# GpSimd's low parts in one instruction of 512 columns, weights released in halves, moments from a sum, and new orders at both ends of a two-block kernel

## The reference, cut to what matters

```
h  = rms_norm(x) * (1 + scale) + shift        # shift, scale, gate: cond @ w_mod
z  = h @ w_in                                  # a_glu, a_val, a_gate, b_q, b_k, b_v, ..., c_gate
u  = conv31(a_val * sigmoid(a_glu)) + b        # 256 channels, one filter of 31 taps each
u  = (u - mean(u)) * rsqrt(mean((u - mean(u))^2) + eps) * ln_w + ln_b   # moments over 256 channels
out = concat(u * gate, window_attention, gated_linear_attention) @ w_out
x  = x + gate * out
```

## Time and profile before

| | before |
|---|---|
| median of 3 runs | 3510.61 us (3509.44 to 3516.84) |
| profiled execution, its own time | 3512.96 us |
| its span, first to last instruction | 3510.8 us |
| mean granted TensorE clock | 0.983 of full speed |
| PE busy | 3364.6 us, 96% of the span |
| DVE / ACT / POOL busy | 60% / 32% / 62% |

### The profile page before, as it was taken

How to read it: one execution, slowest core, us unless ns; L and a number is a source line. 1 busy time by engine, 2 the same in 40 slices (tenths; PEclk the granted TensorE clock), 3 DMA queues, 4 the chain that set the end, 5 groups by cost and what they waited for, 6 DMA issues and landing times.

```text
span 3510.8 us, 51803 instructions
## 1 busy us (share of the span) xinstructions
PE 3364.6 (96%) x19544; PEld 2701.0 (77%) x19544; DVE 2107.1 (60%) x2913; ACT 1131.7 (32%) x1875; POOL 2188.3 (62%) x2500
## 2 busy tenths in 40 slices
PE   5999999999999999999899999998999989999997
PEld 3787688878778777878678888877887768888875
DVE  5684734469652465335766666664534576666666
ACT  4114744221663332232422222233223232222222
POOL 3354433667543578458866667777646886666774
PEclk9999999999999999999999999999999999999998
DMA  5511011332100343224211111123313411111112
GB/s 219 222 60 37 2 37 45 115 125 61 31 21 25 112 147 97 55 67 133 78 43 55 54 55 55 55 79 102 91 55 91 131 58 40 55 55 55 55 37 78
DMA packets 98696, 261.84 MB, mean 75 GB/s; under 512 B 9232, under 2 KB 34832, under 8 KB 97680
## 3 DMA queue, kind: packets, MB, share of 16 engines
q1 hardware_dynamic: 80048, 215.53, 18.5%
q10 hardware_dynamic: 18400, 43.00, 4.2%
HBM read 228.09 MB, written 16.78 MB: 70 GB/s over the span
## 4 chain that ended last, share of the span: by engine, by line
PE 84%; DVE 8%; POOL 3%; ACT 2%; issue 2%; DMA 1%; SPq 0%; ACTq 0%; DVEq 0%; POOLq 0%
PE banks L835 12%; PE banks L837 12%; PE banks L836 12%; PE banks L1376 7%; PE banks L1375 7%; PE banks L1374 7%; PE banks L1414 4%; PE banks L1416 4%; PE banks L1415 4%; PE banks L960 2%; PE banks L977 2%; PE banks L991 2%; POOL w_lo L2977 2%; DVE nt L2266 1%; POOL w_hi L2975 1%
## 5 line engine op out<-in xcount | busy, mean ns | idle before, releaser
L835 PE MATMUL banks<-h_hi,w_hi 128*128 128x512 f32 (+1 forms) x2160 | 838.6, 388 | 20.0 <-POOLq L2982 16.5
L837 PE MATMUL banks<-h_hi,w_lo 128*128 128x512 f32 (+1 forms) x2160 | 818.8, 379 | 0.0
L836 PE MATMUL banks<-h_lo,w_hi 128*128 128x512 f32 (+1 forms) x2160 | 817.7, 379 | 0.0
L2977 POOL TENSOR_TENSOR w_lo<-raw,w_hi 128x256 fp32r<-128x256 f32 x792 | 728.4, 940 | 31.7
L2975 POOL CAST w_hi<-raw 128x512 fp32r<-128x512 f32 x396 | 311.1, 786 | 570.6 <-PE banks L837 407.1
L835 PEld LDWEIGHTS banks<-h_hi,w_hi 128*128 128x128 f32 x2160 | 408.2, 189 | 109.5 <-POOLq L2982 21.3
L836 PEld LDWEIGHTS banks<-h_lo,w_hi 128*128 128x128 f32 x2160 | 408.3, 189 | 82.7 <-issue 6.7
L837 PEld LDWEIGHTS banks<-h_hi,w_lo 128*128 128x128 f32 x2160 | 407.9, 189 | 79.5
L1414 PE MATMUL banks<-g_slot,w_hi 128*128 128x512 f32 x704 | 281.2, 399 | 10.4 <-DVE g_slot L2860 7.3
L1416 PE MATMUL banks<-g_slot,w_lo 128*128 128x512 f32 x704 | 278.8, 396 | 0.0
L1415 PE MATMUL banks<-g_slot,w_hi 128*128 128x512 f32 x704 | 277.9, 395 | 0.0
(11 more groups left out here) (300 smaller groups left out, 6054.2 us busy)
## 6 DMA issues: line engine op xcount, KB each, us to landing
raw<-w_in SPq DMA_DIRECT2D x118, 512.0 KB, 3.5
raw<-w_out SPq DMA_DIRECT2D x64, 512.0 KB, 3.5
pair_y<-w_ffn SPq DMA_DIRECT2D x20, 1024.0 KB, 5.1
raw<-w_ffn SPq DMA_DIRECT2D x20, 1024.0 KB, 5.0
x<-w_mod SPq DMA_DIRECT2D x16, 1024.0 KB, 6.6
wk<-residual ACTq DMA_DIRECT2D x42, 256.0 KB, 2.8
piece<-w_down SPq DMA_DIRECT2D x40, 256.0 KB, 3.0
nt<-w_down SPq DMA_DIRECT2D x40, 256.0 KB, 2.8
```

Source lines behind the costliest of these rows:

```text
L835: mm(o, wh[:, ws], hi[:, kt, t0:t0 + n], start=kt == 0, stop=False)
L836: mm(o, wh[:, ws], lo[:, kt, t0:t0 + n], start=False, stop=False)
L837: last = mm(o, wl[:, ws], hi[:, kt, t0:t0 + n], start=False, stop=kt == nk - 1)
L2977: last = G.tensor_tensor(w_lo[:, piece], raw[:, piece], w_hi[:, piece].bitcast(F32), ALU.subtract)
```

## The change

1. **GpSimd.** The subtract that makes `w_lo` is one instruction of 512 columns where two of 256 stood (L2977 and L3131).
2. **Halves.** `w_split` counts halves: GpSimd raises it after either half, and PE waits for the half that it is to read. In `project` the order is half by half over the token chunks, except for the first block's in-projections (chunk by chunk).
3. **Start.** The parts of `w_mod` are loaded in another order, so that shift and scale of tiles 0 to 3 are complete after two parts. Turns go in pairs into two PSUM banks, DVE's modulation is done in two halves, each followed by its four tiles, and ACT's squares for p1 stand behind all its roundings.
4. **Moments.** In layer 0 of the first block DVE adds the two convolved tiles, and the two squared tiles, before PE's moment matmuls, which are six instead of twelve each time.
5. **End of the feed-forward part.** For the last f, ACT's `take_first` stands ahead of a first tap and a `round_g`, `take_u` behind a first tap; DVE's `low` of the first half stands ahead of the second half's taps, and four additions of the unit down10 p0 are pulled up between the taps.

The diff, cut to its core:

```
-                    for piece in (slice(c, c + 256), slice(c + 256, c + 512)):
-                        last = G.tensor_tensor(w_lo[:, piece], raw[:, piece], w_hi[:, piece].bitcast(F32), ALU.subtract)
+                    last = G.tensor_tensor(w_lo[:, c:c + 512], raw[:, c:c + 512], w_hi[:, c:c + 512].bitcast(F32), ALU.subtract)
+                    if half == 0:
+                        last.then_inc(sem["w_split"], 1)
                 link(last)
...
-                        for c in (0, 256):
-                            part = G.tensor_tensor(w_lo[:, o + c:o + c + 256], src[:, c:c + 256], w_hi[:, o + c:o + c + 256].bitcast(F32), ALU.subtract)
+                        part = G.tensor_tensor(w_lo[:, o:o + 512], src, w_hi[:, o:o + 512].bitcast(F32), ALU.subtract)
...
-                pe.wait_ge(sem["w_split"], g + 1)
+                steps = [(half, ci) for half in range(2) for ci in some]
+                if SEQ[g][0] == "in1":
+                    steps = [(half, ci) for ci in some for half in range(2)]
+                for half, ci in steps:
+                    pe.wait_ge(sem["w_split"], 2 * g + 1 + half)
...
+    START_MOD = [0, 8, 4, 12]
+    TURN_BANKS = [7, 5]
...
-                if u:
-                    turn_modulation(u - 1, 4, mod_row[:, (u - 1) * 512:u * 512], 4 * (u - 1))
+                if u in (1, 3):
+                    turn_modulation(u - 1, 4, mod_row[:, (u - 1) * 512:u * 512], START_MOD[u - 1], u // 2)
                 if u == 1:
                     mean_square(0, 0)
-            turn_modulation(3, 4, mod_row[:, 1536:2048], 12)
+                if u in (1, 3):
+                    turn_modulation(u, 4, mod_row[:, u * 512:(u + 1) * 512], START_MOD[u], u // 2)
...
-            dve.wait_ge(sem["wm_turned"], 4)
-            modulation(0, 0, 16, psum[7][:, 0:32])
-            dve.wait_ge(sem["mod_ready"], 1)
-            tiles(0, 0, range(DT))
+            for half in range(2):
+                dve.wait_ge(sem["wm_turned"], 2 * half + 2)
+                modulation(0, 4 * half, 4 * half + 4, psum[TURN_BANKS[half]][:, 8 * half:8 * half + 8])
+                modulation(0, 8 + 4 * half, 12 + 4 * half, psum[TURN_BANKS[half]][:, 16 + 8 * half:24 + 8 * half])
+                tiles(0, 0, range(4 * half, 4 * half + 4))
...
+                if l == 0:
+                    link(V.tensor_tensor(cv_sq[0][:, 0:end], cv_a[0][:, 0:end], cv_a[1][:, 0:end], ALU.add))
+                    dve.sem_inc(sem["conv_ready"], 1)
...
                 rope(0, at_k)
+                if l == 0:
+                    dve.wait_ge(sem["cstat_ready"], 2)
+                    link(V.tensor_tensor(cv_sq[0][:, 0:end], cv_sq[0][:, 0:end], cv_sq[1][:, 0:end], ALU.add))
+                    dve.sem_inc(sem["cent_ready"], 1)
                 rope(1, at_q[0])
...
-                        last = mm(psum[CONV_BANKS[ci]][:, 0:w], k("ones256"), cv_a[j][:, t0:t0 + w], start=j == 0, stop=j == 1)
+                        last = mm(psum[CONV_BANKS[ci]][:, 0:w], k("ones256"), (cv_a[j] if l else cv_sq[0])[:, t0:t0 + w], start=j == 0, stop=j == l)
...
+                first_tap(NF - 2, 0, 0)
+                first_tap(NF - 2, 1, 0)
+                gate_silu(NF - 2, 0)
+                take_first(NF - 1)
+                first_tap(NF - 2, 0, 1)
+                round_g(NF - 2, 0)
+                gate_silu(NF - 2, 1)
+                first_tap(NF - 2, 1, 1)
+                take_u(NF - 1)
...
+                    if f == NF - 1:
+                        adds += [(len(UNITS) - 3, d, True) for d in range(EARLY_ADDS)]
...
-                    taps_(0)
+                    if f < NF - 1:
+                        taps_(0)
                     low()
+                    if f == NF - 1:
+                        taps_(0)
                     taps_(1)
```

More of the change, by code:

```diff
@@ L823, in project @@
                 _, _, _, nk, chunks, _ = SEQ[g]
-                pe.wait_ge(sem["w_split"], g + 1)
                 wh, wl = w_hi[:, (g % 2) * 1024:], w_lo[:, (g % 2) * 1024:]
-                for ci, (t0, n) in enumerate(chunks):
-                    if only is not None and ci != only:
-                        continue
+                some = range(len(chunks)) if only is None else [only]
+                steps = [(half, ci) for half in range(2) for ci in some]
[3 more added lines that the diff above has]
+                    pe.wait_ge(sem["w_split"], 2 * g + 1 + half)
+                    t0, n = chunks[ci]
                     q = FIRST_CHUNK[g] + ci
-                    if q >= 3:
+                    if q >= 3 and half == 0:
                         pe.wait_ge(sem[f"acc_free{q % 3}"], q // 3)
                     o = (psum_of(q) if bank is None else psum[bank])[:, 0:n]
-                    for kt in range(nk):
+                    for kt in range(4 * half, 4 * half + 4):
                         ws = slice(kt * P, (kt + 1) * P)
@@ L837, in project @@
                         last = mm(o, wl[:, ws], hi[:, kt, t0:t0 + n], start=False, stop=kt == nk - 1)
-                        if kt == 3 and ci == len(chunks) - 1:
-                            last.then_inc(sem["half_used"], 1)
-                    last.then_inc(sem["acc_ready"], 1)
+                    if half:
+                        last.then_inc(sem["acc_ready"], 1)
+                    elif ci == len(chunks) - 1:
+                        last.then_inc(sem["half_used"], 1)
             def project_some(g, ci, k0, k1):
@@ L866, in modulate, with turn_modulation @@
                 last.then_inc(sem["wm_used"], 1)
-            def turn_modulation(n, count, row, m0):
+            def turn_modulation(n, count, row, m0, half=0):
                 pe.wait_ge(sem["wm_copied"], n + 1)
                 for m in range(count):
-                    last = mm(psum[7][:, 2 * (m0 + m):2 * (m0 + m) + 2], row[:, m * P:(m + 1) * P], k("pick"), start=True, stop=True)
+                    last = mm(psum[TURN_BANKS[half]][:, 2 * (m0 + m):2 * (m0 + m) + 2], row[:, m * P:(m + 1) * P], k("pick"), start=True, stop=True)
                 last.then_inc(sem["wm_turned"], 1)
@@ L1523, in _ @@
             copy_row(2)
+            act.wait_ge(sem["mod_ready"], 1)
+            round_h(0, 0, 0)
+            round_h(0, 0, 1)
             copy_row(3)
-            act.wait_ge(sem["mod_ready"], 1)
-            for j in range(4):
+            round_h(0, 0, 2)
+            round_h(0, 0, 3)
+            act.wait_ge(sem["mod_ready"], 2)
+            for j in range(4, DT):
                 round_h(0, 0, j)
             act.wait_ge(sem["x_in1"], 16)
[L1529 to L1532, removed]
+            for d in range(DT):
                 square(0, 1, d, x)
@@ L2181, in _ @@
                 take_c12(F0 + 1)
-                for f in range(F0 + 2, NF):
+                for f in range(F0 + 2, NF - 1):
                     first_tap(f - 1, 0, 0)
@@ L2195, in _ @@
                     take_c12(f)
+                first_tap(NF - 2, 0, 0)
[7 more added lines that the diff above has]
+                take_u(NF - 1)
+                round_g(NF - 2, 1)
+                take_p7(NF - 1)
+                take_c11(NF - 1)
+                take_c12(NF - 1)
                 for h in range(2):
@@ L2834, in add_some @@
                     def add_some():
-                        for n, c in itertools.islice(adds, each):
-                            take_down(n, c)
+                        for n, c, final in itertools.islice(adds, each):
+                            take_down(n, c, final)
                     def taps(m):
@@ L2867, in whole @@
                 def whole(f, n=None):
-                    adds = iter([(n, c) for c in range(U_RESULT[n + 1] - U_RESULT[n])] if n is not None else [])
+                    adds = [(n, c, None) for c in range(U_RESULT[n + 1] - U_RESULT[n])] if n is not None else []
+                    if f == NF - 1:
+                        adds += [(len(UNITS) - 3, d, True) for d in range(EARLY_ADDS)]
+                    adds = iter(adds)
                     each = 2 if f == F0 + 1 else 1
@@ L2881, in whole @@
                     low_()
-                    for n, c in adds:
-                        take_down(n, c)
+                    for n, c, final in adds:
+                        take_down(n, c, final)
                 def take_c22(f):
```

50 lines of the change are left out of this document (29 added, 21 removed).

## The result

The changed kernel takes 3528.77 us (median of 6 runs, 3517.70 to 3529.70), the kernel before 3510.03 (6 runs, 3502.69 to 3516.84). The ratio of the means is 1.0044 with a 95% interval of 1.0025 to 1.0062: it is slower by about 0.44% (0.53% by the medians), where 0.54% faster was forecast. The time lies in the rival that had 0.06 (3523 us): the long subtract costs DVE its critical chains.

The account below looks back on a forecast made before the run. PE, busy 96% of the span, was taken as the bound. Terms −1.6 − 5.0 − 4.25 − 3.7 − 4.4 = −18.95, say −19, from the median 3510.61 gave 3491.6 us; 8 in 10 for 3482 to 3503.

Parts of the forecast that it names:

- the rival that had 0.06: Feed-forward starts and norms: the long subtract costs critical DVE instructions 0.3 us each, net +13, 3523 us; chance 0.06.
- part 1: The 512-wide subtract on POOL: 0.13 us less per half; cost to DVE zero where saturated, 0.145 us each elsewhere.
- Part 6: Other norms and waits: DVE chains beside POOL's splits change by −0 us, within ±2 over all.
- Part 2: Two feed-forward starts: halves let PE start earlier, DVE pays 2 us in the chain; −0.8 each, −1.6 us both.
- Part 3: The start: first half's modulation and tiles come earlier, so norm and later wait shift; −5.0 us.
- Part 4: Moments of layer 0: six matmuls instead of twelve, twice, with DVE's additions covered; −4.25 us.
- Part 5: Two feed-forward ends: PE's waits of 2.31 and 3.64 us go, the second paying partly; −3.7 and −4.4 us.
- the lock: DVE instructions with two SBUF inputs and POOL instructions reading SBUF exclude each other; charged 2 us per feed-forward start.

Follow-up runs that it names:

- e3: The changed kernel with four subtracts of 128 columns instead of one of 512; 3525.33 us, ratio 1.0036 to the kernel before.
- e1: The changed kernel with the subtract back in two instructions of 256 columns everywhere; 3490.31 us, ratio 0.9936 to the kernel before.
- e11: e1 with the copy for the high part of the projections' blocks cut into two of 256; 3491.16 us, ratio 0.9937.
- e8: e1 without halves: PE waits for both halves of a block before its first matmul; 3498.56 us, ratio 0.9963.
- e9: e1 with the feed-forward ends in the order of the kernel before; 3493.83 us, ratio 0.9947.
- e10: e1 with the new orders but no additions of the unit down10 p0 pulled up; 3490.97 us, ratio 0.9935.
- e2: The kernel before with only the 512-wide subtract; 3543.14 us, ratio 1.0084.
- e6: e1 with 512-wide subtracts only in 92 projection blocks (start, norms, feed-forward starts); 3513.09 us, ratio 1.0003.
- e7: e1 with four subtracts of 128 in 15 blocks (start, layer 1's norms, second layers' start); 3495.54 us, ratio 0.9950.

## Why the prediction was wrong

**The step that failed is in part 1**: "On average that is zero where DVE is saturated (what it loses is POOL's time in total, 1.28 for 1.41)". It took POOL's work in a stretch as fixed. But DVE's work in a critical stretch is what is fixed, a number of tiles, and POOL, which had a backlog, does as many turns beside it as DVE has instructions. The price of a DVE instruction is then set by POOL's mean turn. POOL's instructions, min, median and max ns, in the changed kernel, e3, e1 and e11:

```profile
L3019 POOL TENSOR_TENSOR w_lo<-raw,w_hi x396: 1262/1300/3227, 35.6 to 2843.4; 128x512 fp32r<-128x512 f32 x198
L3018 POOL CAST w_hi<-raw x396: 606/613/3195, 34.9 to 2842.2; 128x512 fp32r<-128x512 f32 x198
```

```profile
L3020 POOL TENSOR_TENSOR w_lo<-raw,w_hi x1584: 445/462/2511, 35.1 to 2848.0; 128x128 fp32r<-128x128 f32 x198
```

```profile
L3020 POOL TENSOR_TENSOR w_lo<-raw,w_hi x792: 717/742/2782, 35.1 to 2816.4; 128x256 fp32r<-128x256 f32 x198
```

```profile
L3018 POOL CAST w_hi<-raw x396: 386/398/2172, 34.3 to 2812.6; 128x256 fp32r<-128x256 f32 x198
```

Mean turn from the minima, and half of a tile (one DVE instruction):

```
                          POOL's turns of a half     mean turn   DVE instruction
four subtracts of 128     0.61 + 4 x 0.445            0.48        0.90
two of 256, copy cut      2 x 0.386 + 2 x 0.717       0.55        0.98
two of 256                0.61 + 2 x 0.717            0.68        1.12
one of 512                0.61 + 1.262                0.93        1.42
```

From the first row to the last the turn grows by 0.45 us and the DVE instruction by 0.52; the two rows between lie on that line within 0.02. That is 0.30 us for each DVE instruction from 256 to 512, the very price that the rival used. The table is one norm, two to five tiles of each run, in which neither engine rests for long. The Trainium skill's rule (SBUF — State Buffer, "Who interferes with whom") holds in this trace for two SBUF inputs, and L2859 with one kept 689 ns. By these records the two engines don't exclude each other over the whole of an instruction: a DVE instruction that doesn't wait for POOL takes 0.75 us, and in each row of the table it is some 0.3 us shorter than 0.75 and the mean turn together. I had cited the rule, and then averaged its effect away.

**Part 6, other norms, "−0, within ±2"**, falls with it. In the changed kernel some 17 us were lost outside the start, the moments, and the feed-forward starts and ends (16.9 in all, less −1.1, −0.9, +3.6, +3.3, −0.8 and −4.3 from the places). In e1 the same stretches are 3.9 us ahead.

**Part 2, −1.6 for the feed-forward starts.** In the changed kernel it was +6.9; in e1 −3.3. The mechanism stood as written: the wait for weights goes and a chain of ACT and DVE binds behind it. Only the tiles ahead of that chain had become 0.6 us longer each and the four long additions later still, so the chain ended 12.3 us after PE was free. Halves alone are worth about 6 us there (e8).

**Part 3, the start, −5.0.** In e1 −4.6: right. In the changed kernel −1.1: PE's norm matmul came at 59.92 us and not at 55.7 (56.23 in e1). Counted from the first matmul of each execution that is 41.6 us, and 38.5 in e1. The longer turns, which tiles beside POOL's first splits pay, are not all of the 3.1 between them: PE's second group of `w_mod` matmuls took 3.37 us in the changed kernel's execution and 1.92 in e1's, ahead of POOL's first split (34.87 us). In e9, with the subtract in two, that group took 3.64, and the norm matmul came at 39.7. So some 1.9 us are the subtract's, and 1.2 vary from one execution to another; e9's start shows −3.3 for the place, so the closeness of e1's −4.6 is in part its execution's luck. PE's timeline in the changed kernel, and in e1 the wait that was forecast for 76.1:

```profile
59.92 1.56 PE L903 MATMUL banks<-nt,cst 128*128 128x512 f32 x4 [1.21 <-DVE nt L2280]
80.60 0.77 PE L793 MATMUL banks<-h_hi,w_hi 128*128 128x512 f32 x1 [6.83 <-ACTq L1566]
```

```profile
76.59 0.76 PE L793 MATMUL banks<-h_hi,w_hi 128*128 128x512 f32 x1 [6.62 <-ACTq L1566]
```

**Part 4, the moments, −4.25**: right in both. In e1 the place shows −4.0; in the changed kernel it shows −0.9, but 3.1 us were lost near 180 us to a stretch at half clock (last section), ahead of the moments. The chain of the changed kernel, against the earlier trace rows:

```profile
257.57 2.15 PE banks L947 x6
...
273.54 2.15 PE banks L953 x6
```

No idle time stands before them, so DVE's two additions are covered, as said.

**Part 5, the ends, −3.7 and −4.4.** The named waits went, but DVE's additions took 5.9 of 6.8 us back at the first end and 4.7 at the second. e9 puts the moves at 0.7 and 2.2 us. The term was mis-sized: of the second wait I let PE keep a third, and DVE's pace takes nearly all. The four pulled-up additions do nothing (e10). In e1 the ends win 2.1 and 4.9 in all, but more than half of that e9 wins too, with the old orders. There the granted clock fell to half in the profiled execution of the kernel before, and less of it in the others; windows of the same matmuls behind the first wait of the second end, before and in e9:

```profile
3424.00:3429.00 5.00, 5.00 (x16) 3.93 (x16) 2.96 (x5) 2.57 (x5) 1.30 (x2) 0.66 0.00 0
```

```profile
3407.00:3412.00 5.00, 4.92 (x21) 4.05 (x22) 3.45 (x5) 2.37 (x5) 2.07 (x3) 1.00 0.00 0
```


Without what part 2 charged for the lock (2 us at each start) the sum was −23, and e1 measured −22.9 (3490.31 against 3513.22 for the kernel before in the same runs). That agreement is partly luck: by terms it is −5.6 forecast and −3.3 found at the feed-forward starts, −8.1 and −7.0 at the ends (of which the moves give 2.9), 0 and −3.9 elsewhere. The edit that I costed at nothing outside the starts decided the sign. In the chances, the list of rivals leaves 0.85 for faster and 0.06 for slower where the sentence behind it has 0.86 and 0.05; nothing hangs on it.

## What to carry to other kernels

Where DVE and GpSimd alternate on SBUF without a rest, don't cost a longer GpSimd instruction by GpSimd's total: each DVE instruction with two SBUF inputs on the critical path grows with GpSimd's mean turn. Cut GpSimd's instructions short where DVE is waited for, and only as far as GpSimd itself isn't late (128 columns everywhere cost nearly as much here as 512). A time that can be won on the bounding engine at one place is worth what the next engine's pace leaves of it, so compare that pace before counting a wait as won.

## What was not expected of the hardware

In the kernel before and in e1 the clock stays full after a pause of PE of 1.1 us near 180 us; in the changed kernel, with the same pause, it falls to half (1.2 of 2.4 GHz). The pause, in the changed kernel and in e1 (in brackets):

```profile
181.46 0.61 PE L881 MATMUL banks<-cst,wk 128*128 128x2 f32 x4 [1.15 <-ACT wk L1583]
```

```profile
177.35 0.61 PE L881 MATMUL banks<-cst,wk 128*128 128x2 f32 x4 [1.14 <-ACT wk L1583]
```

Windows of that stretch, of the changed kernel and of e1 (PE's granted clock is the number behind POOL's):

```profile
175.00:200.00 25.00, 23.85 (x153) 19.17 (x152) 24.19 (x30) 3.23 (x7) 5.94 (x5) 0.86 0.32 106
```

```profile
175.00:200.00 25.00, 23.86 (x145) 19.47 (x146) 23.48 (x28) 3.08 (x7) 11.88 (x10) 1.00 0.32 106
```

0.86 over 25 us is some 7 us at half. PE was as busy in both and lost some 3.1 us there in the changed kernel. e2, e3, e6, e7 and e8 had it too, in e3 for a shorter while, the others not; what decides it is open. It may be a part of the spread between runs, but only one execution of each kernel was profiled. Differences of 3 us between kernels here should be read by places, not by spans.
